# First two tiles of a two-block kernel: high parts of the input ahead of its squares, products in operand order, products of ones in front

## What is computed

```python
def rmsnorm(x, g):
    xf = x.astype(jnp.float32)
    y = xf * lax.rsqrt(jnp.mean(xf * xf, axis=-1, keepdims=True) + EPS)
    return (y * g.astype(jnp.float32)).astype(x.dtype)
...
        u = rmsnorm(h, norm_in[i])
        proj = u @ w_in[i]
        (m_q, m_k, m_v, m_o, m_z, m_if, a_q, a_k, a_v, a_z,
         ix_q, ix_k, ix_w) = jnp.split(proj, SPLIT_POINTS, axis=-1)
```

## Time and profile before

| | us |
|---|---|
| median of 3 runs | 1637.16 |
| lowest and highest run | 1635.53, 1640.14 |
| the profiled execution | 1638.42 |
| its span | 1636.6 |
| TensorE busy in it | 1615.0 |
| VectorE, ScalarE, GpSimd busy | 1048.2, 733.8, 663.8 |

### The profile page before, as it was taken

How to read it: one execution, slowest core, us unless ns; L and a number is a source line. 1 busy time by engine, 2 the same in 40 slices (tenths; PEclk the granted TensorE clock), 3 DMA queues, 4 the chain that set the end, 5 groups by cost and what they waited for, 6 DMA issues and landing times.

```text
span 1636.6 us, 22469 instructions
## 1 busy us (share of the span) xinstructions
PE 1615.0 (99%) x7955; PEld 1279.3 (78%) x7955; DVE 1048.2 (64%) x1672; ACT 733.8 (45%) x1274; POOL 663.8 (41%) x307
## 2 busy tenths in 40 slices
PE   7999999999999999999999999999999999999999
PEld 6688777777888888777778877777788888888887
DVE  6599686677336877777775077876766765665100
ACT  5433365565345645544553244444524444343210
POOL 4244564323454344344464332222144354444442
PEclk9999999999999999999999999999999999999999
DMA  6233321214333244211113321111233233233331
GB/s 210 65 118 101 91 78 54 75 52 141 91 103 103 65 135 131 70 52 52 52 60 96 90 73 57 52 54 50 87 118 99 77 103 103 90 103 92 101 96 59
DMA packets 40408, 143.25 MB, mean 88 GB/s; under 512 B 4729, under 2 KB 5209, under 8 KB 39937
## 3 DMA queue, kind: packets, MB, share of 16 engines
q1 hardware_dynamic: 37600, 131.96, 26.5%
q10 hardware_dynamic: 2720, 10.11, 1.7%
HBM read 137.57 MB, written 4.48 MB: 87 GB/s over the span
## 4 chain that ended last, share of the span: by engine, by line
PE 49%; DVE 1%; ACT 1%; issue 0%; ACTq 0%; DVEq 0%
PE bank L767 10%; PE bank L769 9%; PE bank L768 9%; PE bank L1420 4%; PE bank L1419 4%; PE bank L1421 4%; PE bank L1305 2%; PE bank L1326 1%; PE bank L1314 1%; PE bank L1273 1%; PE bank L1281 0%; ACT w_hi L1441 0%; ACT gm L1981 0%; PE bank L788 0%; PE bank L789 0%
## 5 line engine op out<-in xcount | busy, mean ns | idle before, releaser
L632 POOL TENSOR_TENSOR w_lo<-w_raw,w_hi 128x1024 fp32r<-128x1024 f32 x243 | 597.5, 2462 | 938.0 <-ACT w_hi L1441 800.5
L767 PE MATMUL bank<-u_hi,w_hi 128*128 128x512 f32 x776 | 332.0, 428 | 1.4 <-ACT gm L1981 0.8
L769 PE MATMUL bank<-u_hi,w_lo 128*128 128x512 f32 x776 | 305.3, 393 | 0.0
L768 PE MATMUL bank<-u_lo,w_hi 128*128 128x512 f32 x776 | 304.7, 393 | 0.0
L1441 ACT ACTIVATE w_hi<-w_raw 128x1024 fp32r<-128x1024 f32 x199 | 209.4, 1056 | 210.3 <-PE bank L769 169.7
L767 PEld LDWEIGHTS bank<-u_hi,w_hi 128*128 128x128 f32 x776 | 146.7, 189 | 43.4 <-issue 11.4
L768 PEld LDWEIGHTS bank<-u_lo,w_hi 128*128 128x128 f32 x776 | 147.1, 190 | 32.8 <-issue 4.6
L769 PEld LDWEIGHTS bank<-u_hi,w_lo 128*128 128x128 f32 x776 | 146.8, 189 | 32.3
L1419 PE MATMUL bank<-u_hi,w_hi 128*128 128x512 f32 x288 | 112.0, 389 | 0.0
L1420 PE MATMUL bank<-u_lo,w_hi 128*128 128x512 f32 x288 | 112.0, 389 | 0.0
L1421 PE MATMUL bank<-u_hi,w_lo 128*128 128x512 f32 x288 | 112.0, 389 | 0.0
(11 more groups left out here) (476 smaller groups left out, 3436.9 us busy)
## 6 DMA issues: line engine op xcount, KB each, us to landing
w_raw<-weights SPq DMA_DIRECT2D x243, 512.0 KB, 3.6
xt<-x_t SPq DMA_DIRECT2D x8, 256.0 KB, 6.6
hank<-bias_dram ACTq DMA_DIRECT2D x8, 256.0 KB, 4.0
xt<-x_t ACTq DMA_DIRECT2D x1, 2048.0 KB, 8.4
h_dram<-h_res ACTq DMA_DIRECT2D x1, 2048.0 KB, 7.7
h_res<-h_dram ACTq DMA_DIRECT2D x1, 2048.0 KB, 7.5
out<-h_res SPq DMA_DIRECT2D x8, 256.0 KB
p_val<-p_t ACTq DMA_DIRECT2D x1, 512.0 KB, 10.6
```

The source lines that it names most:

```text
L632: pool.tensor_tensor(w_lo[:, j, :], w_raw[:, j, :], w_hi[:, j, :].bitcast(F32), ALU.subtract).then_inc(w_lo_ready, 1)
L767: pe.matmul(o, hi, xh, start=(i == 0), stop=False)
L768: pe.matmul(o, hi, xl, start=False, stop=False)
L769: mm = pe.matmul(o, lo, xh, start=False, stop=(i == n - 1))
```

## The change

On TensorE five products of ones with ones (128 x 512, plain float32) are issued first, into bank 4. Then `column_tile` gives way for q0 and q1 to single products, each waiting for what it alone needs: high weight x high input (`high`) for w_hi and xg_hi, low weight x high input (`low_weight`) for w_lo, high weight x low input (`low_input`) for xg_lo. Their order is written out: all of q0's first parts, q1's without its low weights, parts 4 to 7, q1's low weights, and the low inputs of parts 4 to 7 last. `token_sums` moves behind q2's part 0, `spread_scale` behind its part 3. On ScalarE all eight high parts come first, then chunk 2's high part, then the eight squares, then chunk 3's. On VectorE all eight low parts come before the six additions.

```diff
--- before.py
+++ after.py
@@ -829,17 +829,65 @@
                 return xg_hi[:, k, :], xg_lo[:, k, :]
 
             q0, q1, q2, q3 = st["idx_q"]
-            for t in (q0, q1):
-                column_tile(t, of_xg, 0, (0, 4), xg_lo_ready)
+
+            def high(t, k):
+
+                c, s = t["parts"][k]
+                pe.wait_ge(xg_hi_ready, k + 1)
+                pe.matmul(bank[t["bank"]][:, :], w_hi[:, c % RING, s * P:(s + 1) * P], xg_hi[:, k, :], start=(k == 0),
+                          stop=False)
+
+            def low_weight(t, k):
+
+                c, s = t["parts"][k]
+                return pe.matmul(bank[t["bank"]][:, :], w_lo[:, c % RING, s * P:(s + 1) * P], xg_hi[:, k, :],
+                                 start=False, stop=(t is q1 and k == KD - 1))
+
+            def low_input(t, k):
+
+                c, s = t["parts"][k]
+                pe.wait_ge(xg_lo_ready, k + 1)
+                return pe.matmul(bank[t["bank"]][:, :], w_hi[:, c % RING, s * P:(s + 1) * P], xg_lo[:, k, :],
+                                 start=False, stop=(t is q0 and k == KD - 1))
+
+            pe.wait_ge(ones_ready, 1)
+            for k in range(5):
+                pe.matmul(bank[4][:, :], ones[:, 0:P], ones[:, :], start=True, stop=True)
+            pe.wait_ge(w_hi_ready, q0["parts"][0][0] + 1)
+            high(q0, 0)
+            high(q0, 1)
+            pe.wait_ge(w_lo_ready, q0["parts"][0][0] + 1)
+            for k in (0, 1):
+                low_weight(q0, k)
+            for k in (2, 3):
+                high(q0, k)
+                low_weight(q0, k)
+                low_input(q0, k - 2)
+            for k in (2, 3):
+                low_input(q0, k)
+            pe.wait_ge(w_hi_ready, q1["parts"][0][0] + 1)
+            for k in range(4):
+                high(q1, k)
+                low_input(q1, k)
             for k in range(4, KD):
-                column_tile(q0, of_xg, 0, (k, k + 1), xg_lo_ready)
-                column_tile(q1, of_xg, 0, (k, k + 1), xg_lo_ready)
-                if k == 6:
-                    pe.wait_ge(ones_ready, 1)
-                    token_sums(lambda k: sq[:, 0, :], lambda k: sq[:, 1, :])
+                high(q0, k)
+                low_weight(q0, k)
+                high(q1, k)
+            pe.wait_ge(w_lo_ready, q1["parts"][0][0] + 1)
+            for k in range(4):
+                low_weight(q1, k)
+            for k in range(4, KD):
+                mm = low_input(q0, k)
+                if k == KD - 1:
+                    mm.then_inc(dense_done, 1)
+                low_input(q1, k)
+                mm = low_weight(q1, k)
+            mm.then_inc(dense_done, 1)
             column_tile(q2, of_xg, part=(0, 1))
+            token_sums(lambda k: sq[:, 0, :], lambda k: sq[:, 1, :])
+            column_tile(q2, of_xg, part=(1, 4))
             spread_scale(0, 5)
-            column_tile(q2, of_xg, part=(1, 8))
+            column_tile(q2, of_xg, part=(4, 8))
             column_tile(q3, of_xg)
             column_tile(st["idx_k"][0], of_xg)
             pe.wait_ge(consts_in, 16 * 3)
@@ -1530,6 +1578,8 @@
                 if i % 4 == 0:
                     split_weights(i // 4 - RING)
                 act.activation(xg_hi[:, i, :], x_tile(i), ACT.Copy, scale=vec("norm_in", i)).then_inc(xg_hi_ready, 1)
+            split_weights(2 - RING)
+            for i in range(KD):
                 square_part(i, xt[:, i, :], sq[:, 0, :], u_val, sq[:, 1, :])
             split_weights(-1)
             token_std(bank[4][:, 0:NT], 0)
@@ -2227,8 +2277,8 @@
                 dve.wait_ge(xg_hi_ready, i + 1)
                 dve.scalar_tensor_tensor(xg_lo[:, i, :], xt[:, i, :], vec("norm_in", i), xg_hi[:, i, :].bitcast(F32),
                                          ALU.mult, ALU.subtract).then_inc(xg_lo_ready, 1)
-                if 1 <= i < KD - 1:
-                    add_part(sq[:, 0, :], u_val[:, (i - 1) % 2, :], i == 1)
+            for i in range(1, KD - 1):
+                add_part(sq[:, 0, :], u_val[:, (i - 1) % 2, :], i == 1)
             scales()
             dve.wait_ge(norm_spread, 1)
             link(dve.tensor_copy(r_in[:, :], bank[5][:, :]))
```

## The result

| | before | changed |
|---|---|---|
| median of 20 runs, us | 1638.38 | 1640.57 |
| lowest and highest | 1635.49, 1640.46 | 1637.34, 1643.83 |
| the profiled execution's span | 1636.6 | 1640.6 |
| TensorE busy in it | 1615.0 | 1625.0 |

The changed kernel is slower: ratio 1.0016, interval 1.001 to 1.0022, that is 1.6 to 3.6 us. The forecast was 1637.2 in a range of 1633.8 to 1640.2, so the time lies 0.4 us above its upper end. Over twenty runs the kernel before itself lies 1.2 us above the 1637.16 from which the forecast set out; the other 2.2 are the change's.

The account below looks back on a forecast made before the run. The prediction took TensorE's work plus its waits to bound the kernel. Its terms, -3.9 (way to q2) + 2.8 (new wait) + 1.2 (clock) = +0.1, put the median of 1637.16 at 1637.2 us, range 1633.8 to 1640.2.

Parts of the forecast that it names:

- ones over: TensorE's five products of ones at the start: end at 7.3 to 9.5 us, 8.3 taken.
- the wait: TensorE behind q2's part 0, held until the last addition of squares: from 20.6 to 23.4, 2.8 us.
- the slow first products: TensorE's first products at the lower clock level: cost almost nothing, since what follows waits for 15.40 anyway.
- TensorE's own order: Products in the order of their operands on TensorE's way to q2: a gain of 3.9 us.
- the landing of chunk 2: ScalarE before the squares: idle from 14.0 until chunk 2 lands at 15.7, squares only after its split at 16.75.
- sixteen one-column products: The norm's sums on TensorE: 1.7 us with almost no columns through the array, beside the 2.8 us wait.
- the sum: All terms for the whole kernel: -3.9 + 2.8 = -1.1, with + 1.2 for the clock +0.1.
- the term of the clock: TensorE's clock around the wait and sums: one fall, partly inside the wait, 1.2 us lost; ends zero and 2.5.
- third rival: Slower: clock low beyond the spread, 1638.5, or one more addition caught by GpSimd plus the fall, 1639.5; chance 0.17.
- within 0.3%: Whole kernel's time within 4.9 us of before: chance 0.90, with faster and slower 0.05 each.
- second rival: The sums aren't late, TensorE has only its own work: -3.9 up to -4.9, 1632.3 to 1633.3; chance 0.12.

Follow-up runs that it names:

- y2: x4 without the five products of ones in front; ratio 0.9988 to the kernel before.
- x5: The kernel before with the five products of ones put in front and nothing else; ratio 1.0008 to the kernel before.
- y4: The changed kernel's order on ScalarE and VectorE only, TensorE as in the kernel before; ratio 1.0026 to the kernel before.
- x4: The changed kernel's TensorE order, ones included, with ScalarE and VectorE as in the kernel before; ratio 0.9987 to the kernel before.
- x7: The changed kernel with three of the eight squares moved ahead of chunk 2's high part on ScalarE; ratio 1.0017 to the kernel before.
- x1: The changed kernel with three more products of ones between q2's part 0 and the sums on TensorE; ratio 1.0006 to the kernel before.
- x2: The changed kernel with the sums behind q2's part 3 and the spread behind part 5; ratio 0.9996 to the kernel before.
- y3: x2 with the low input of x tile 3 issued behind the high parts of tiles 4 and 5; ratio 1.0001 to the kernel before.
- y1: The changed kernel as it is, run again for a second profile; ratio 1.0020 to the kernel before.
- x8: x4 with the high part of x tile 7 made ahead of the square of tile 6; ratio 0.9999 to the kernel before.

## Why the prediction was wrong

Most steps held. Predicted and measured, in us: ones over by 7.3 to 9.5, and 7.5; GpSimd's chunk 1 done at 13.7, and 14.0; the last high part 14.0, and 13.8; squares from 16.75, and 16.5; TensorE at the sums at 20.6, and 21.0 to 21.2; sums ready at 23.4, and 23.6; the wait 2.8, and 2.46. That the slow first products cost nothing (y2, x5), that the new order of ScalarE and VectorE makes the sums late (y4), and that TensorE's own order gains (x4), is each shown. One cause in it was weighed too heavily: the landing of chunk 2, named as what stands ahead of all squares, is worth 0.6 us (x7); the rest is six additions behind eight low parts and a GpSimd operation. The "sixteen one-column products" are eight, recorded as sixteen instructions; the time taken for them is right. Without the clock the sum gives -1.1; x1, where it holds, has q2's part 4 at 28.42 against 29.26, so -0.8.

The step that failed is the term of the clock: its mechanism was right, its size was not. I took 1.2 us, from one fall of 3.5 us partly hidden in the wait, with 2.5 as the upper end. In the profile it cost 2.91 (31.33 less 28.42), 3.18 by by_bucket, and in the second 1.5; over the runs it is 7.0 us more at the lower level, 2.5 us of time at 0.36 each, 3.2 by the price of this stretch. Two assumptions were wrong in it. The low stretch didn't begin inside the wait, where it would have been free, but at 25.1 or 25.7, behind it, when TensorE was busy again. And it can last 6.8 us, though TensorE works in it, which no row of before shows (the fall of the earlier trace rows lasted 3.5). With 3.2 in place of 1.2 the sum is +2.1, from x1's -0.8 it is +2.4, and 2.2 to 2.6 were measured. The third rival's first price, 1638.5 or +1.4, was the nearest, and that rival (the clock stays low beyond the spread) is what happened; it had 0.17.

The rule that I weighed, the Trainium skill's (TensorE: Matmul & The Clock Gate, "Why this matters for your kernels") against idle gaps between bursts, pointed the right way. The trace agrees with it in kind (2.46 us of wait, then the fall at 25.1), but not in size: the gaps that it warns of are longer than this one and than the 2.34 us of x2, and in y3 the clock fell behind a wait of only 1.08 us next to one-column products. The advice to warm up, which the prediction took from the same place, stands there for measuring, and y2 against x4 shows nothing gained by it.

The range failed for a second reason: it was built round a median of three runs, and the kernel's own scatter, by chance falls of the clock after 900 us, moved that median by 1.2 us. The same scatter hides what the prediction called "about what a measurement can tell", 4.9 us: the change is 2 to 3 us and was told apart by twenty runs. As for the signs, the chance of 0.90 for within 0.3% fits, but there was a direction in it, and the forecast of +0.1 gave none.

The second rival, in which the sums aren't late, is what x4 and y2 are, once ScalarE and VectorE stay as they were: 0.9988 without the ones, 2 us faster than the kernel before and some 5 us faster than the changed one.

## What to carry to other kernels

A wait put next to many tiny products costs more than its length: price the clock behind it, at the full length of a low stretch, and fill the wait with products that are ready, or better, keep what feeds it early. Making an operation earlier is no gain by itself where VectorE and GpSimd both read from SBUF: ask which of the other's operations it will now meet. And where the clock falls by chance elsewhere, compare kernels by many runs and by their time at the lower level, not by two profiles.

## What the runs showed of the hardware

- The clock rises under plain float32 products of ones as it does under others: the five in front took 6.0 us in all (1.47 to 7.46), where by estimate, from 0.85 us each at the upper level, they would take 4.3 there alone and 8 at the lower. Behind them parts of q0 start 0.23 us apart (9.78, 10.01, 10.24), and 0.43 apart without them (y2: 9.89, 10.32, 10.75). This is read from the distances; the profile's granted clock is 1.00 in both.
- TensorE's granted clock can be at half level for 6.8 us while its busy time is 6.80 of 6.80, after a stretch of 4.2 us in which it was busy for 1.74. y4 and x7 have such a stretch too, y1 and y3 one of 3.4 us.
- Next to one-column products a shorter wait was enough for a fall, 1.08 us in y3, than between full products, where the clock held behind 1.85 us in x5 and fell behind 2.34 us in x2; each is from one profile.
- VectorE operations with two SBUF inputs that meet GpSimd's 2.4 us operation take 2.8 to 2.9 us in place of 0.74 (2.86 in the earlier trace rows, 2.92 in x2, 2.87 in x8), and a start 0.3 us earlier or later decides which operation it is: in the changed kernel the low part of x tile 3 starts at 10.95, ahead of GpSimd's 11.12, and takes 0.74, while the next one takes 2.83 from 11.69; in x2 it starts at 11.30, with GpSimd's 11.31, and takes 2.92.
- Of the scatter of the runs of one kernel, 1635.1 to 1642.0 us over 103 runs of the kernel before, nearly all goes with the time at the lower level (correlation 0.95, 0.36 us for each us).
